# Which engine makes the low parts of the weights while the expert choice is decoded

## The reference

```python
q = (hb @ w_query).reshape(t, PEER_HEADS, 2, PEER_HALF)
s = jnp.einsum('thpc,hpnc->thpn', q, sub_keys)
v1, i1 = lax.top_k(s[:, :, 0], PEER_TOPK)
v2, i2 = lax.top_k(s[:, :, 1], PEER_TOPK)
cand = (v1[..., :, None] + v2[..., None, :]).reshape(t, PEER_HEADS, PEER_TOPK * PEER_TOPK)
...
best, pos = lax.top_k(cand, PEER_TOPK)
experts = jnp.take_along_axis(cand_idx, pos, axis=-1)
gate = jax.nn.softmax(best, axis=-1)
...
act = jax.nn.gelu(jnp.einsum('thkd,td->thk', u, hb), approximate=False)
return jnp.einsum('thk,thkd->td', gate * act, vsel)
```

## Time and profile before

| | |
|---|---|
| time, median of 3 runs | 1673.73 us (1673.41 to 1675.66) |
| the profiled execution | 1670.86 us, span 1669.1 us |
| TensorE matmul busy | 1612.8 us (97%) |
| VectorE busy | 1248.2 us (75%) |
| ScalarE busy | 966.6 us (58%) |
| GpSimd busy | 72.7 us (4%), 64.9 us of it 27 low parts of 2402 ns |
| a low part on VectorE | 1225 ns |

### The profile page before, as it was taken

How to read it: one execution, slowest core, us unless ns; L and a number is a source line. 1 busy time by engine, 2 the same in 40 slices (tenths; PEclk the granted TensorE clock), 3 DMA queues, 4 the chain that set the end, 5 groups by cost and what they waited for, 6 DMA issues and landing times.

```text
span 1669.1 us, 25849 instructions
## 1 busy us (share of the span) xinstructions
PE 1612.8 (97%) x9816; PEld 1378.7 (83%) x9816; DVE 1248.2 (75%) x1984; ACT 966.6 (58%) x1342; POOL 72.7 (4%) x46
## 2 busy tenths in 40 slices
PE   7999989998999999999999999999998989999997
PEld 2777779998999888888888888888888778888886
DVE  3668766999888999987777666776667887676666
ACT  5545755555555555555555555665556767665556
POOL 0000007520000000000000000000000000000000
PEclk9999899999999999999999999999999999999999
DMA  8654235445665555576665665455544543555552
GB/s 344 252 174 157 99 106 197 172 170 196 215 194 188 208 212 206 214 253 226 217 213 198 218 215 182 147 205 200 182 170 164 202 135 139 191 208 189 194 187 76
DMA packets 53262, 317.79 MB, mean 190 GB/s; under 512 B 5937, under 2 KB 6097, under 8 KB 19218
## 3 DMA queue, kind: packets, MB, share of 16 engines
q1 hardware_dynamic: 51954, 310.08, 52.3%
q0 software_dynamic: 1184, 6.05, 1.0%
HBM read 306.65 MB, written 9.47 MB: 189 GB/s over the span
## 4 chain that ended last, share of the span: by engine, by line
PE 80%; DVE 13%; ACT 4%; issue 1%; DMA 1%; SPq 0%; DVEq 0%; ACTq 0%
PE pb L933 79%; DVE w_lo L2096 4%; DVE ar L2096 3%; ACT ar L1609 2%; DVE ar L2108 2%; DVE ar L2510 1%; ACT w_hi L1609 1%; DVE ar L2507 1%; DMA raw<-in_wall 1%; ACT L1609 1%; DVE ar L2514 1%; DVE ar L2282 0%; DVE ar L2112 0%; DVE sm L2360 0%; PE pb L1248 0%
## 5 line engine op out<-in xcount | busy, mean ns | idle before, releaser
L2096 DVE TENSOR_TENSOR w_lo<-raw,w_hi 128x1024 fp32r<-128x1024 f32 x471 | 577.1, 1225 | 175.6 <-ACT w_hi L1609 143.6
L1609 ACT ACTIVATE w_hi<-raw 128x1024 fp32r<-128x1024 f32 x498 | 528.7, 1062 | 139.1 <-PE pb L933 98.3
L933 PE MATMUL pb<-HX,w_hi 128*128 128x256 f32 (+1 forms) x2768 | 507.6, 330 | 7.8 <-DVE ar L2096 3.3
L933 PEld LDWEIGHTS pb<-HX,w_hi 128*128 128x128 f32 x2768 | 413.6, 191 | 49.1 <-DVE ar L2096 3.7
L933 PE MATMUL pb<-w_hi,HC 128*128 128x512 f32 (+1 forms) x1648 | 445.5, 391 | 2.6 <-DVE HC L2108 1.7
L933 PEld LDWEIGHTS pb<-w_hi,HC 128*128 128x128 f32 x1648 | 301.3, 188 | 63.0 <-issue 3.4
L1609 ACT ACTIVATE ar<-pb 128x256 f32<-128x256 f32 (+2 forms) x320 | 152.6, 477 | 303.0 <-PE pb L933 201.8
L933 PE MATMUL pb<-HX,w_lo 128*128 128x256 f32 x1952 | 279.0, 284 | 2.9 <-DVE w_lo L2096 2.7
L2096 DVE TENSOR_TENSOR ar<-ar 128x512 f16<-128x512 f16 (+8 forms) x441 | 246.8, 588 | 43.2 <-ACT ar L1609 19.9
L933 PEld LDWEIGHTS pb<-HX,w_lo 128*128 128x128 f32 x1952 | 263.5, 192 | 15.0 <-DVE w_lo L2096 3.7
L933 PE MATMUL pb<-w_lo,HC 128*128 128x512 f32 (+1 forms) x824 | 254.9, 388 | 0.0
(11 more groups left out here) (148 smaller groups left out, 673.9 us busy)
## 6 DMA issues: line engine op xcount, KB each, us to landing
raw<-in_wall SPq DMA_DIRECT2D x257, 1024.0 KB, 4.8
ar<-in_wmod SPq DMA_DIRECT2D x24, 512.0 KB, 4.3
act_keep<-ar SPq DMA_DIRECT2D x28, 256.0 KB, 5.5
ar<-act_keep SPq DMA_DIRECT2D x28, 256.0 KB, 5.0
x<-in_wmod SPq DMA_DIRECT2D x8, 512.0 KB, 5.6
ar<-in_bigrows POOLq DMA_DIRECT2D x2, 1024.0 KB, 4.9
ar<-acs_keep POOLq DMA_DIRECT2D x2, 1024.0 KB, 8.6
x<-in_x SPq DMA_DIRECT2D x1, 1024.0 KB, 11.1
```

Of the source, the lines that this page charges most:

```text
L933: return e.matmul(o, l, r, start=start, stop=stop, skip_group_check=True)
L1609: a.did(e.activation(out, in_, func, scale=scale, **kw), sig)
L2096: v.did(e.tensor_tensor(out, a_, b_, op), sig)
```

## The change

GpSimd makes the low parts of all units from 52 to 92, without a hole: 69, 70, 76 to 83 and 89 to 92 come to it from VectorE (14 units). Its two waits for VectorE's low parts go, as there is no change of hands any more until VectorE takes over at unit 93.

```diff
-LO_POOL = (set(range(U_QUERY + 4, U_PEER + 5)) | set(range(U_PEER + 7, U_PEER + 12))
-           | set(range(U_PEER + 20, U_PEER + 25)))
+LO_POOL = set(range(U_QUERY + 4, U_PEER + 29))
...
                     if w in LO_POOL:
-                        if w in (U_PEER + 7, U_PEER + 20):
-                            p.wait_ge(*LOW[w - 1])
                         p.wait_ge(s_hi, made + 1)
                         p.settle()
                         p.did(e.tensor_tensor(w_lo[:, made % NH, :], raw_half(w),
```

## The result

The change makes the kernel slower: 1693.66 us median (1692.93 to 1694.73) against 1674.7 us, ratio 1.0116, 95% interval 1.0104 to 1.0128. The profiled execution took 1692.93 us. Its page answers to the earlier trace rows; the last line is GpSimd's group of low parts.

A forecast was written before the change was run, and what follows sets the result against it. TensorE bounds the kernel, VectorE the decoding. Waits of 43 us, less low parts shed, delay the transpose by 25.4 us; with 1.6 for the clock, +27: 1697.9 profiled, median 1701, range 1666 to 1714 (own range 1690 to 1716).

The forecast's parts named there:

- turn-taking: VectorE's two-input operations and GpSimd's parts wait for each other's whole instructions during decoding; 1701 us, chance 0.60.
- The unknown cost: First decoded block: VectorE's two-input operations wait for GpSimd's parts, 17 waits of 2.53 us, 43 us.
- Block 1 runs free: Second decoded block: GpSimd has nearly made its 23 parts, so VectorE works without waits, 31.6 us, to 417.0.
- The 2.7 us stay: Behind the transpose of the choice: TensorE still waits 2.7 us for VectorE's one-hots.
- the clock costs 1.6 more: After TensorE's pause its matmuls run at the lower clock level for a while, adding 1.6 us.
- The sum to the one-hots: Transpose of the choice 25.4 us later, plus 1.6 for the lower clock: +27 us.
- The two removed waits bring nothing by themselves.: GpSimd's waits for VectorE's low part: 10.1 us of GpSimd idle time that nobody waited for.
- ScalarE's exponential: Second block's, near 405 us, holds back unit 93's high part; first block's, 8 to 12 us late, stalls TensorE.
- A sign: VectorE's eight adds at the start of decoding take over 12 us instead of 2.77.
- Rival 1: During decoding VectorE and GpSimd do not feel each other; gain 6.8 us, to 1667; chance 0.23.
- Rival 2: During decoding both engines halve their rate while both read; 1676 us, chance 0.09.
- Rival 3: During decoding VectorE has precedence and GpSimd's low parts come late; 1677 us, chance 0.08.

The follow-up runs named there:

- two_halves: The changed kernel with each GpSimd low part made by two subtractions of 512 columns; 1685.43 us, ratio 1.0071.
- write_only: The changed kernel with GpSimd's subtraction replaced by two memsets, so it reads nothing and units 52 to 92 get zero low parts; 1666.2 us, ratio 0.9954.
- no_waits: The kernel before with only GpSimd's two waits for VectorE's low part removed, no part changing hands; 1686.76 us, ratio 1.0081.
- exp_later: The changed kernel with ScalarE's exponential of block 1 one chunk later; 1694.83 us, ratio 1.0126.

## Why the prediction was right, and where it was off

It forecast slower by turn-taking, 1701, and measured are 1693.7, inside the forecast's own range. The mechanism is the one that it named; two of its terms came right in part by luck. Its steps:

- **The unknown cost.** Turn-taking of whole instructions holds: the surplus of 2.1 us whatever the size, `two_halves`, `write_only`. The sum of the waits in block 0 was set at 17 x 2.53 = 43 us. It is 39.3 (312.26 to 382.40 is 70.1, less 30.8 of work): some 19 waits of 2.07 (row by row they add up to 39.9). That the term is off by only 3.7 us is in part luck, as two errors cancel. The price was too high: a wait is shorter than GpSimd's pitch of 2.53, since a part is 2.40 and the operation begins after it (352.24 against 352.07). The two-input operations had 16 waits, 34.1 us, not 43. And three of the 19 were operations with one input (a cast, two tensor_scalars, 5.7 us), which the prediction had not counted at all. The adds went two to a part as assumed, but in `chosen`, where GpSimd's parts came without a pause, each short operation waited by itself.
- **Block 1 runs free.** Right: 31.2 us for 31.6. The margin was small, and here too it had luck: GpSimd's last part ends at 381.8 and block 1's cast begins at 382.40. In `two_halves` the order is the other way round, and the adds lose 8.7 us.
- **"The 2.7 us stay", and the clock costs 1.6 more.** The stretch behind the decoding is as long as before, 8.74 us, so its first half is right. The second is wrong: the sum put the slow clock behind VectorE's lateness, and they lie beside each other, TensorE being slow while it would have waited. The term should have been nothing.
- **The sum to the one-hots.** +27.0 were forecast and +21.9 measured: 3.7 less waits, 0.4 less in block 1, 1.6 less for the clock, and 0.6 more that the decoding began late.
- **"The two removed waits bring nothing by themselves."** Wrong in what it means for the kernel: `no_waits` costs 13 us. Nobody waited for GpSimd there, but its idleness was what kept the adds free. The total holds all the same since the turns of the adds were counted.
- **ScalarE's exponential** of block 1 stood at 401.35 (forecast 405), and the pause before unit 93 was 17.7 us (forecast 15 to 20); that it is only the place where the lateness shows is borne out by `exp_later`. The stall of a few us that was forecast in block 0 didn't come: its exponential ran at 341.74, 4.3 us later than before and not 8 to 12, and TensorE kept its pitch of 2.88 us up to 385. The total doesn't hang on it.
- **A sign.** The adds were to take over 12 us and took 11.62; what was meant by it, the waits, is there.
- **From the profile to the median.** 2.9 us were added for the distance of the profiled execution from its median; for the changed kernel it is 0.7. That is 2.2 us of the 7.

Rival 1 fell as a forecast; its price, 1667, is close to what `write_only` gives, 1666.2. Rival 2 (a shared rate) is excluded by `two_halves` and by the constant surplus. Rival 3 (VectorE first) fell with the adds at 11.62 us.

## What to carry to other kernels

Before work goes to GpSimd, look at what VectorE does in the same microseconds: beside MAX8, FIND_INDEX8, MATCH_REPLACE8 and reductions a GpSimd subtraction was free, while two-input operations, casts and tensor_scalars waited for it in turn. Short ones lost the most for their size: 2.1 us on an operation of 0.29. A wait in front of such a run of GpSimd may look idle and be what makes the run free; try it alone before it goes. And where an engine's wait moves when the order is changed while the time stays, as in `exp_later`, it was not the cause.

## What the hardware showed unexpectedly

- VectorE operations with one input wait beside GpSimd too: a tensor_scalar of 128x8 took 1.99 us instead of 0.17, one of 128x128 2.44 instead of 0.23, a cast of 128x512 2.12 instead of 0.43. The same kinds wait even beside a memset (1.06, 1.14), which the two-input operations don't. The Trainium skill, SBUF — State Buffer, section "Who interferes with whom", has both halves: two inputs contend with GpSimd's reads only, while cast and tensor_scalar can run in two-port modes, which contend with its instructions whether they read or not. The runs agree. The Trainium skill, Advanced Engine Details and Errata, section "Mode Summary", names the two-port modes alone; the adds at 11.62 us, which are tensor_tensor, decide against taking it as the whole rule.
- The wait is inside the recorded duration on both engines, so a busy VectorE (1271.2 us after, 1248.2 before, with 14 operations fewer) hides it; no idle time points there.
